# Closing each run of gathered row groups with its own weights, and TensorE summing one group behind instead of two

## The reference, cut to what matters

```python
g = jax.nn.softmax(top, axis=-1).astype(xb.dtype)
act = jax.nn.gelu(jnp.einsum('tped,td->tpe', u[eidx], xb), approximate=False)
return jnp.einsum('tpe,tped->td', g * act, v[eidx])
```

## Time and profile before

| | |
|---|---|
| three runs | 2582.58, 2589.87, 2590.87 us, median 2589.87 |
| the profiled execution, its own time | 2584.61 us |
| its span, first to last instruction | 2582.8 us |
| TensorE busy, weight loads busy | 1893.1 us, 1092.7 us |
| VectorE busy | 1842.7 us |
| ScalarE busy | 603.7 us |
| GpSimd busy | 854.9 us |
| moved by DMA | 958.16 MB, of them 805.36 MB gathered rows |
| mean rate, best slice | 371 GB/s, 422 GB/s |

### The profile page before, as it was taken

One profiled execution on the slowest core, in us unless ns is written; L12 is line 12 of the kernel. 1 busy time (PEld: TensorE's weight loads), 2 busy tenths in 40 slices (PEclk: granted clock), 3 DMA queues, 4 the chain that ended last, 5 costly groups with the idle time before them and its releaser, 6 DMA issues. The chain is left out here.

```text
span 2582.8 us, 23078 instructions
## 1 busy us (share of the span) xinstructions
PE 1893.1 (73%) x6726; PEld 1092.7 (42%) x6726; DVE 1842.7 (71%) x4563; ACT 603.7 (23%) x1668; POOL 854.9 (33%) x772
## 2 busy tenths in 40 slices
PE   7883876887777657776877767679777766677575
PEld 6771653664344223343543334347444422232222
DVE  3338968847877992357679866998787789677765
ACT  2213233313111221123222221342211122211121
POOL 0012232322433331234333323343344344344442
PEclk8987887987989777788988879899898888888888
DMA  9848897888998998899899979899999999999996
GB/s 405 335 116 336 349 377 300 336 347 340 402 374 352 417 386 361 341 379 421 359 417 421 421 302 371 329 394 362 394 414 399 386 421 422 421 397 422 421 422 270
DMA packets 140128, 958.16 MB, mean 371 GB/s; under 512 B 18148, under 2 KB 20836, under 8 KB 24804
## 3 DMA queue, kind: packets, MB, share of 16 engines
q0 software_dynamic: 110592, 805.36, 76.6%
q1 hardware_dynamic: 23024, 147.01, 14.5%
q10 hardware_dynamic: 6388, 4.33, 0.5%
HBM read 953.75 MB, written 2.89 MB: 370 GB/s over the span
## 5 line engine op out<-in xcount | busy, mean ns | idle before, releaser
L731 PE MATMUL acc<-rows,diag 128*128 128x512 f32 x2136 | 1154.6, 691 | 459.2 <-ACT diag L924 458.8
L662 POOL DMA_INDIRECT rows<-in_uv,eidx x768 | 854.6, 1113 | 1689.3 <-PE acc L731 1243.3
L1215 DVE CUSTOM_DVE_ANT_0 rows<-rows,xb 128x1024 f32<-128x1024 f32 x768 | 916.4, 1221 | 251.9 <-DMA rows<-in_uv,eidx 251.3
L731 PEld LDWEIGHTS acc<-rows,diag 128*128 128x128 f32 x2136 | 451.4, 221 | 1076.0 <-ACT diag L924 581.3
L924 ACT ACTIVATE act_out<-act_in 128x2 f32<-128x2 f32 x384 | 78.1, 203 | 1419.3 <-DVE act_in L1215 1407.3
L1204 DVE SCALAR_TENSOR_TENSOR side<-rows,wv,side 128x1024 f32<-128x1024 f32 x234 | 300.5, 1284 | 8.3
L680 PE MATMUL bank<-wt,hT 128*128 128x256 f32 x944 | 213.4, 387 | 10.2 <-ACT hT L924 7.4
L924 ACT ACT_TABLE_LOAD x139 | 178.3, 1283 | 126.5 <-DVE act_in L1215 31.7
L680 PEld LDWEIGHTS bank<-wt,hT 128*128 128x128 f32 x944 | 183.6, 195 | 44.6 <-ACT hT L924 9.4
L924 ACT ACTIVATE diag<-small,wv 128x128 f32<-128x128 f32 x534 | 191.8, 387 | 0.0
L680 PE MATMUL bank<-hT,wt 128*128 128x256 f32 (+1 forms) x960 | 183.1, 353 | 6.1 <-ACT hT L924 3.8
(11 more groups left out here) (179 smaller groups left out, 1330.3 us busy)
## 6 DMA issues: line engine op xcount, KB each, us to landing
wt<-in_ada_w SPq DMA_DIRECT2D x32, 1024.0 KB, 10.2
wt<-in_peer_w_q SPq DMA_DIRECT2D x26, 1024.0 KB, 9.6
rows<-in_ada_w SPq DMA_DIRECT2D x16, 1024.0 KB, 22.7
wt<-in_mlstm_w_in SPq DMA_DIRECT2D x15, 1024.0 KB, 9.0
rows<-in_uv,eidx POOLq DMA_INDIRECT x768, 12.9
wt<-in_attn_w_qkv SPq DMA_DIRECT2D x12, 1024.0 KB, 8.9
rows<-in_mlstm_w_in SPq DMA_DIRECT2D x9, 1024.0 KB, 27.5
wt<-in_attn_w_out SPq DMA_DIRECT2D x8, 1024.0 KB, 9.7
```

The costliest lines, as they stand in the source:

```text
L662: nc.gpsimd.indirect_dma_start(out=rows[:, r, :], out_offset=None, in_=A["uv"], in_offset=bass.IndirectOffsetOnAxis(ap=eidx[:, b, slot:slo ...
L731: last = nc.tensor.matmul(acc[:, h * 512:(h + 1) * 512], diag[:, r, :], rows[:, r, D + h * 512:D + (h + 1) * 512], start=first and j == 0, ...
L1215: last = V.tensor_tensor_reduce(out=rows[:, r, 0:D], in0=rows[:, r, 0:D], in1=xb[:, place, :], scale=1.0, scalar=0.0, op0=ALU.mult, op1=AL ...
```

## The change

A run now closes itself. `last_groups`, called once at a block's end, becomes `end_of_run`, called at the end of every run. The body gets a flag, `opens`, that is true for the first group of a run.

- VectorE: at a run's end it waits for the Gelu of the run's last group, and does that group's weights and side addition. The first body of a run does dots only.
- ScalarE: at a run's end it waits for these weights and makes the last group's diagonals. The first body of a run does the Gelu only.
- TensorE: body n sums group n - 1, in every run. At a block's end one group is left instead of two. Before a step of the trunk it has therefore one more group to sum, and one fewer behind it.
- The loop begins after the run's first group, so a run needs thirteen groups or more to have one; before it was twelve. No run of this plan has as many, and one, the last, has twelve.

```diff
-        def run_groups(eng, s, body, last_ones):
+        def run_groups(eng, s, body, end_of_run):
...
-                    body(order, n, g * GS, n % RING, n // RING, g)
-
-            g = lo
-            if g < 3:
-                straight(g, min(3, hi))
-                g = min(3, hi)
+                    body(order, n, g * GS, n % RING, n // RING, g, False)
+
+            g = min(max(lo + 1, 3), hi)
+            body(order, base + lo, lo * GS, (base + lo) % RING, (base + lo) // RING, lo, True)
+            straight(lo + 1, g)
             whole = (hi - g) // RING
...
             straight(g, hi)
-            if hi == GROUPS:
-                last_ones(order, base + GROUPS)
+            end_of_run(order, base + hi, hi)
...
-            def group(order, n, slot, ring, turn, g):
-                if g == 2 and n >= GROUPS:
+            def group(order, n, slot, ring, turn, g, opens):
+                if g == 1 and n >= GROUPS:
 
                     pe.wait_ge(sum_read, n // GROUPS)
-                if g is None or g >= 2:
-                    add_up(order, n - 2, (ring - 2) % RING, g == 2)
-
-            def last_groups(order, n):
-                add_up(order, n - 2, (n - 2) % RING, False)
-                add_up(order, n - 1, (n - 1) % RING, False)
+                if g != 0:
+                    add_up(order, n - 1, (ring - 1) % RING, g == 1)
+
+            def end_of_run(order, n, hi):
+                if hi == GROUPS:
+                    add_up(order, n - 1, (n - 1) % RING, False)
...
-            def group(order, n, slot, ring, turn, g):
+            def group(order, n, slot, ring, turn, g, opens):
                 act.wait_ge(dots, n + 1)
                 f(act_out[:, ring, :], act_in[:, ring, :], ACT.Gelu).then_inc(gelus, 1)
-                if g != 0:
+                if not opens:
                     diagonals(order, n - 1, (ring - 1) % RING)
 
-            def last_groups(order, n):
+            def end_of_run(order, n, hi):
                 diagonals(order, n - 1, (n - 1) % RING)
...
                     last.then_inc(dots, 1)
-                    if g != 0:
+                    if not opens:
                         weigh(b, n - 1, slot - GS, (ring - 1) % RING)
                         if has_side(order, (ring - 1) % RING):
                             add_up(n - 1, (ring - 1) % RING)
                 return body
 
-            def last_groups(b):
-                def body(order, n):
-                    weigh(b, n - 1, SLOTS - GS, (n - 1) % RING)
+            def end_of_run(b):
+                def body(order, n, hi):
+                    weigh(b, n - 1, (hi - 1) * GS, (n - 1) % RING)
                     if has_side(order, (n - 1) % RING):
                         add_up(n - 1, (n - 1) % RING)
                 return body
```

More of the change, by code:

```diff
@@ L621, in run_groups @@
                         n = base + g + k
-                        body(order, i * RING + n, i * (RING * GS) + (g + k) * GS, n % RING, i + n // RING, None)
+                        body(order, i * RING + n, i * (RING * GS) + (g + k) * GS, n % RING, i + n // RING, None, False)
                 g += whole * RING
             straight(g, hi)
-            if hi == GROUPS:
-                last_ones(order, base + GROUPS)
+            end_of_run(order, base + hi, hi)
         block = ctx.enter_context(nc.Block())
@@ L761, in _ @@
                 if k == "GROUPS":
-                    run_groups(pe, s, group, last_groups)
+                    run_groups(pe, s, group, end_of_run)
                     continue
@@ L974, in _ @@
                 if k == "GROUPS":
-                    run_groups(act, s, group, last_groups)
+                    run_groups(act, s, group, end_of_run)
                     continue
@@ L1207, in group, with body @@
             def group(b, place):
-                def body(order, n, slot, ring, turn, g):
+                def body(order, n, slot, ring, turn, g, opens):
                     if g == 0:
@@ L1252, in _ @@
                         dve.wait_ge(experts_chosen, QUARTERS * GORDER.index((s[1], s[2])) + 1)
-                    run_groups(dve, s, group(s[2], GORDER.index((s[1], s[2])) % 2), last_groups(s[2]))
+                    run_groups(dve, s, group(s[2], GORDER.index((s[1], s[2])) % 2), end_of_run(s[2]))
                     continue
```

## The result

| | before | after |
|---|---|---|
| runs | 2582.58 to 2591.98 us, 4 runs | 2624.52 to 2629.64 us, 4 runs |
| median | 2590.37 us | 2626.16 us |
| ratio, 95% interval | | 1.0146 [1.0123, 1.0169] |
| profiled execution | 2584.61 us, span 2582.8 | 2629.64 us, span 2627.8 |

The change makes the kernel 36 us slower. The forecast was 2610 us, with a range of 2552 to 2634.

The account below looks back on a forecast made before the run. Several stretches were taken as bound by VectorE and its round trips, later ones by a full gather queue. From the profiled 2584.6 us, +35 + 7 - 16 = +26 gave 2610 us; range 2552 to 2634, the forecast's own 2594 to 2634.

Parts of the forecast that it names:

- the bound of the first block: Stretches such as 218 to 480 us are bound by VectorE and its round trips to ScalarE and TensorE, not by gathers.
- (a): At run ends VectorE waits for ScalarE's Gelu, mainly in one-group runs of stretches it bounds: +35 us of 46.6.
- (c): TensorE sums one group more before each trunk step, costing where its result is awaited: +7 us, bounds 0 and 30.
- (b): Five MOD steps, 970 to 1100 us: VectorE's Gelu waits replace its waits for TensorE's columns: 0, or 50 us uncovered.
- (d): Ring slots come free one group sooner, so gathers fill some holes of the DMA engines: -16 us.
- R1: Faster rival: the ring was the limit and one more group's transfer fills each DMA hole; 2555 us, chance 0.25.
- (e): At run ends ScalarE waits 0.4 us for the weights; VectorE stands in the same wait, so not counted twice.
- R3: Much slower rival: MOD waits uncovered, run-end Gelu waits not absorbed; 2673 us, or 2648 with half the MOD cost; chance 0.05.
- R2: No-change rival: half-absorbed Gelu waits plus later trunk steps, against a slot gain of 30 us; 2585 us, chance 0.17.
- wv waits: VectorE's weight instruction waiting for ScalarE's Gelu output: from 23.6 us in 9 waits to over 100 waits, 60 to 140 us.
- GpSimd's wait: GpSimd's wait for TensorE's sums before refilling a ring slot, 1243.3 us before, should fall by over 100 us.
- group 58 of the first block: Sign of the forecast: VectorE should reach this group some 15 us later than in the kernel before.

Follow-up runs that it names:

- 1: close_only: the changed kernel with TensorE again summing two groups behind, so runs close without the earlier sums; 2611.97 us, ratio 1.0104.
- 9: The changed kernel with TensorE taking the extra sum only where a run opens, staying two groups behind within runs; 2588.19 us, ratio 0.9968.
- 5: The changed kernel measured again, unedited, on one chip beside other runs; 2634.9 us, ratio 1.015 to the kernel before.
- 6: close_multi: the kernel before with only runs of two groups or more closed, TensorE two groups behind; 2589.47 us, ratio 0.9981.
- 3: The kernel before with VectorE only waiting at each run's end for the last group's Gelu, no work moved; 2595.99 us, ratio 1.0047.
- 4: The kernel before with GpSimd waiting for one sum more before refilling a slot, a ring one group shorter; 2661.8 us, ratio 1.03.

## Why the prediction was right, and where its terms were off

The sign and the range held, and the bound of the first block was read rightly: by stretch, from the waits and not from the busy share. The measured terms, in the order closing (1), sums at openings (9 against 1), sums within runs (5 against 9), are +27, -35 and +47 us. Together they are +39. My sum had +35, -16 and +7, together +26. Closing was off by 8 us, the sums at openings by 19, and the sums within runs by 40, more than the whole forecast. The last two errors point opposite ways and cancelled in part. That is luck: with the gain of 16 as predicted, the other two as measured make +58 us, 2643, beyond the range. The upper end of the forecast's own range doesn't follow from its words either: (a) and (c) in full and a gain of 16 are 2645 us, not 2634.

**(a) held in size, but not in place.** I had +35 of 46.6 us. Closing cost 27 us over before, and its one-group runs 32 us (1 against 6). The price of a wait held too. VectorE's waits after, in the matches of 218 to 480 and of 1640 to 1820:

```profile
DVE wv L1197 <- ACT act_out L922: 17.2, 30, 2.0
...
DVE wv L1197 <- ACT act_out L922: 18.1, 26, 1.6
```

The prediction had 19.4 us in 29 waits and 20.4 in 25. From dots to weights is 0.27 to 0.35 us in most one-group runs and 1.61 to 1.74 in most with a table load, where I took 0.4 and 1.7. The further drain of some 1380 ns that the Trainium skill gives (page "ScalarE: Activation LUTs", section "What ACT_TABLE_LOAD costs") isn't there. What I had wrong is where it is absorbed and where it lasts. The 18 us lost up to 672 were all taken back in the wait for rows from 672 to 813 (close_only); I had counted most of them as lasting. In return 10 us were lost from 1120 to 1552, where I had called the waits hidden. The price of one wait was right; that the total came so near was in part luck.

**(b) held**: 68.2 us of waits in place of 69.3, and the stretch no longer (3).

**(c) failed, and is the step that was wrong.** The prediction wrote that "in runs of several groups TensorE must also wait until VectorE has the last group's dots", and then priced the step by the sum's matmuls, 1.7 or 3.5 us, at the few places where the result is awaited. The wait got no price. It puts TensorE's trunk step behind VectorE's, by 10.84 us at one place, and with the sum behind it costs 47 us in all (9). The upper bound that I set, 30 us, was also made of sums only. Two signs stood in the earlier trace rows. TensorE is idle for 8.34 us, waiting for diagonals just ahead of PQ, even when it is two behind. And the eight matmuls after that take 6.03 us, not the 3.5 that I took from the 24 in 10.46.

**(d) was mis-sized.** -16 predicted, -35 measured (9 against 1). I counted single holes that a wait for rows follows. The shorter ring (4) shows that a slot's worth is spread over everything from 1120 on: in the stretch from 1120 to 1552 the sums at openings bring 23 us (441.6 to 418.3), in the others 1 to 6 us or a loss of 1 to 2. In that stretch VectorE's wait for rows falls from 47.5 us in close_only to 32.2, which is 15 of the 23. R1's mechanism is thus real. It was outweighed, where R1 expected VectorE's round trips to be absorbed.

**(e)** ScalarE's wait for the weights, 72.6 us in 168 places, was counted at nothing beside VectorE's. No run here separates it; close_multi has 43.4 us of it in 45 places and is no slower than before.

**R3** didn't occur: MOD stayed covered. **R2**, 2585 us by a gain of 30 from the slots, had the gain nearly right and missed the wait in (c).

Of the signs: wv waits in over 100 places held (163), but 194.8 us was over the 60 to 140 named. That range lay below the prediction's own terms: 46.6, 12 and 68 us, and the 23.6 of before, are 150. The rest is in waits that no term had, the longest of them 15.19 us at the MOD step of the first block (586.05 to 601.24). GpSimd's wait fell by 69 us, not by over 100, and 49 went to the side sums. VectorE reached group 58 of the first block 27 us later, 5 of which stood at the first dots already. The one more sum ahead of the PQ of the earlier trace rows is seen at 742.40, with 6.47 us of idle before it; at the next PQ it is seen at 799.72, with the 10.84 us. The profiled execution after was 19 us above the sum's 2610.6.

## What to carry to other kernels

A lag between engines is not only latency: it lets each be at a different step of a hand-written order. Before an engine is moved one item closer to its producer, look up after which instruction of the producer this item is made. If that is a later item, the engine inherits the wait for all the work in front of it, and the price to work out is that of the two steps run in turn, beside the item's own duration. The useful half of such a change, taking what is already finished when a run opens, is often free of that wait and can be made alone.

In this kernel a short round trip cost time in the runs where nothing stands between the request and its use (122 runs, 32 us), and none in those where an independent instruction does (84 runs); so close the runs that have such work, and leave the others open. Even an uncovered wait costs nothing if a longer wait for something else follows, as from 672 to 813.

## What the runs showed of the hardware beyond that

One group less in a ring of six costs 78 us of 2590 (3%) in a kernel whose DMA engines are already busy nine tenths of nearly every slice. Of the 120 us by which VectorE's waits for rows grew, about two thirds reached the end. And two edits that each look like less latency, closing and summing sooner, gave +27 and +94 us alone but +39 together. Their costs don't add: closing makes the diagonals of a one-group run before the sum asks for them.

TensorE came back slower from a wait: eight matmuls right behind an idle time of 10.84 us took 6.30 us, at a granted clock of 0.50 until 804.90, against 3.70 us for eight at 1.00.
